# Delta-net projection by seven products: another order of the products, turned signs, and a bank of its own for two of them

## The chip, the cores and the metric

The kernel runs on one core of one Trainium2 chip. The number that counts is the device time of one execution in microseconds. A core has TensorE (matrix products, weight loads beside them), VectorE, ScalarE and GpSimd, and in the profile they are called PE (PEld for the weight loads), DVE, ACT and POOL. Products land in eight PSUM banks of 128 partitions and 512 fp32 numbers, called B[0] to B[7]; all else lies in SBUF. The engines wait for one another by counting semaphores.

## The reference

The kernel computes two blocks of a first model (a gated delta-net mixer and a retention mixer, each with a convolved feed-forward part) and a third block of another kind. The change touches only the delta-net mixer, and there the input projection of each of eight heads:

```python
def gated_deltanet(h, w_in, conv_w, a_log, dt_bias, norm_w, w_out):
    proj = h @ w_in                                  # h: 512 tokens x 1024
    qkv, z, a, bt = jnp.split(proj, ...)
    qkv = jax.nn.silu(causal_dwconv(qkv, conv_w))
    q, k, v = jnp.split(qkv, [H * dk, 2 * H * dk], axis=-1)
    ...                                              # decays, q and k normalised
    sol = lax.linalg.triangular_solve(kk + eye, rhs, lower=True, unit_diagonal=True)
    ...                                              # chunks of 64: state, output o
    o = o * lax.rsqrt(jnp.mean(o * o, ...) + 1e-6) * norm_w * jax.nn.silu(z)
    return o.reshape(b_, s, H * dv) @ w_out
```

All of it is fp32.

## The kernel before, in words

**The projection of a head.** A head needs four blocks of 128 output columns (q, k, v, z) of 1024 inputs for 512 tokens. They are made two at a time: pair (h, 0) is q and k, pair (h, 1) is z and v. A pair is a 2x2 product of blocks: weights A11, A12 (first block, lower and upper 512 inputs) and A21, A22 (second block), against the tokens' halves. Instead of eight block products it makes seven, M1 to M7, in Winograd's form. Each is four matmuls (128 inputs each) of 256 tokens. What the form needs beside them:

- sums of the weights, S1 to S4, which GpSimd makes in place in the ring of weight slots (`pool_gdn`; lines 2213, 2220, 2223 and 2225 are S3, S2, S1 and S4, 128x512 each);
- sums of the inputs, T1 to T4 (`gdn_T[0..3]`), made once by VectorE at the start (lines 1953 to 1964);
- copies of M1 and M7 out of their banks by ScalarE (`keep_m1` line 1694, `keep_m7` line 1701) and of the finished quarter C11 (`keep_c11`, line 1708), since M2 and M4 are added on top of M1 and M7 in the bank;
- the sums of the results by VectorE (`dve_pair`): t (line 1919), U2 (1926), c21 (1932), c22 (1937), c12 (1944).

**The order.** `GDN_ORDER` gives the order of the seven products; with four matmuls each a pair has steps 0 to 27 and a head 0 to 55. `pe_steps` issues a range of them and, at the first step of a product, the waits. The steps are not issued in one piece. They fill TensorE's gaps while it works on an earlier head, by hand-written positions:

- In the opening (`pe_gdn`, lines 1477 to 1542) pair (0,0) and (0,1) run among small products that make the gates, the first key sum (line 1510), the key products `kk` (1516), the transpose (1523), `qk` (1531) and `ktok` (1541). Steps 0 to 13 of pair (1,0) stand there too, the last two right in front of the head loop.
- In the head loop, each head h inverts its triangular matrix in six levels. A level is LD (line 1605), Tm on VectorE (2075), TE (line 1617), the inverse's update and transpose on VectorE (2091, 2093). Seven steps of head h+1 stand in each level, from step 14 on, split as `fill` says. So pair (h+1, 0) ends in level 2 and pair (h+1, 1) runs through levels 3 to 6.
- Then comes the state's recurrence over four pieces (lines 1653 to 1670: kv, wS, o) with the steps 0 to 13 of head h+2 between, as `ahead` says. VectorE makes vn (line 2170) and S (2184) for it, and between them it does convolution taps (1906), the next head's L (2016) and first D (2028, 2032).

The four columns of an adaLN product (`pe_ada`, line 256) stand in level 1 of every head but the first, in bank 7. ScalarE and VectorE have their orders written out as well (`act_gdn`, `dve_gdn`). GpSimd per head: S3 of the pairs (h+1,1) and (h+2,0), the other three of (h+1,1), one product on XT (line 2249), two decays, the other three of (h+2,0), and the query's product (2243). In the opening it waits, ahead of the sums of (1,0), for the first inverse of head 0 (VectorE, line 2041):

```python
            third(1, 0)
            decay(0)
            pool.wait_ge(dve_done, at("dve", "gdn", "inv", 0, 0))
            others(1, 0)
            query(0)
```

## Time and profile before

| what | us |
|---|---|
| device time, median of 3 runs | 2595.95 (2595.76 to 2597.06) |
| span of the profiled execution | 2595.1 |
| TensorE busy | 2532.1 (98%) |
| VectorE busy | 1643.4 (63%) |
| ScalarE busy | 719.3 (28%) |
| GpSimd busy | 252.9 (10%) |
| first and last start of a product of the pairs (line 1467) | 43.7 and 399.4 |
| one head of the loop (TensorE's line 1647, 164.70 to 211.85) | 47.15 |

The profiled execution is one execution; the page gives its span, which is 0.85 us under the median. The change touches the stage from some 40 to 402 us. A row of a timeline is a group of like instructions one after another: its start, the time from start to end, the engine and line of the kernel, what it writes and reads, and in brackets the time that the engine stood idle before it and what ended this.
### The profile page before, as it was taken

How to read it: one execution, taken by the hardware profiler on the slowest of the kernel's cores; microseconds unless marked ns; L12 is line 12 of the kernel's file. 1: busy time of each engine (PE TensorE's matmuls, PEld its weight loads, DVE VectorE, ACT ScalarE, POOL GpSimd, SP SyncE). 2: the span in 40 equal slices, each digit the busy share in tenths (PEclk: the TensorE clock that was granted, in tenths of full speed). 3: DMA queues.
4: the chain of work that ended last, by engine and by line, in shares of the span. 5: the costliest groups of instructions: out<-in, count | busy, mean ns of one | idle time of the engine just before them, and what ended most of it. 6: DMA issues, size and time to landing. Idle time of an engine off the chain costs nothing.

```text
span 2595.1 us, 32921 instructions
## 1 busy us (share of the span) xinstructions
PE 2532.1 (98%) x13038; PEld 1999.9 (77%) x13038; DVE 1643.4 (63%) x2905; ACT 719.3 (28%) x1381; POOL 252.9 (10%) x186
## 2 busy tenths in 40 slices
PE   6999999999999999999999999999999999999999
PEld 3777775688888888888888888886445568888888
DVE  2787875687776365455648777745375486666652
ACT  3555553321110122211203111004253375222200
POOL 1434331100000030000001000001121000000000
PEclk9999999999999999999999999999999999999999
DMA  8222311243433321122023453331021310212121
GB/s 350 109 79 74 131 74 72 91 185 146 188 142 144 120 77 70 69 83 84 33 97 130 163 195 148 137 122 69 33 83 65 130 66 33 93 70 98 67 90 55
DMA packets 26377, 276.81 MB, mean 107 GB/s; under 512 B 3689, under 2 KB 4585, under 8 KB 9201
## 3 DMA queue, kind: packets, MB, share of 16 engines
q1 hardware_dynamic: 23040, 268.92, 27.1%
q10 hardware_dynamic: 3184, 5.78, 0.7%
q8 instruction: 105, 1.72, 0.3%
q14 instruction: 48, 0.39, 0.0%
HBM read 272.58 MB, written 2.11 MB: 106 GB/s over the span
## 4 chain that ended last, share of the span: by engine, by line
PE 87%; DVE 7%; ACT 3%; DMA 2%; issue 1%; POOL 0%; SPq 0%; ACTq 0%; DVEq 0%; POOLq 0%
PE bank L688 29%; PE bank L772 15%; PE bank L2583 11%; PE bank L1467 5%; PE bank L2996 5%; PE bank L2369 4%; PE bank L419 3%; DVE arena L1906 1%; PE bank L2674 1%; DMA arena<-w_ada 1%; PE bank L501 1%; PE bank L2989 1%; PE bank L1617 1%; PE bank L1605 1%; PE bank L3139 1%
## 5 line engine op out<-in xcount | busy, mean ns | idle before, releaser
L688 PE MATMUL bank<-HT,ring 128*128 128x256 f32 x1056 | 248.0, 380 | 2.0 <-ACT HT L1104 2.0
L688 PE MATMUL bank<-arena,ring 128*128 128x256 f32 x1056 | 249.5, 379 | 0.0
L688 PE MATMUL bank<-arena 128*128 128x256 f32 x1056 | 249.5, 379 | 0.0
L688 PEld LDWEIGHTS bank<-HT,ring 128*128 128x128 f32 x1056 | 199.3, 190 | 34.2 <-issue 5.2
L688 PEld LDWEIGHTS bank<-arena,ring 128*128 128x128 f32 x1056 | 200.6, 190 | 27.3
L688 PEld LDWEIGHTS bank<-arena 128*128 128x128 f32 x1056 | 200.6, 190 | 27.3
L772 PE MATMUL bank<-arena,ring 128*128 128x256 f32 x936 | 207.0, 379 | 1.4 <-ACT arena L845 1.4
L772 PEld LDWEIGHTS bank<-arena,ring 128*128 128x128 f32 x936 | 177.4, 190 | 27.1 <-ACT arena L845 2.6
L1328 ACT ACTIVATE arena<-bank,ffc 128x512 f32<-128x512 f32 x66 | 51.3, 777 | 487.3 <-DVE bank L1234 487.3
L1133 POOL TENSOR_SCALAR XT<-XT,comb_v 128x512 f32<-128x512 f32 x32 | 50.1, 1577 | 1049.3 <-ACT HT L1104 652.3
L2996 PE MATMUL bank<-HT,ring 128*128 128x512 f32 x320 | 146.5, 598 | 0.5 <-ACT HT L1145 0.5
L1467 PE MATMUL bank<-arena,ring 128*128 128x256 f32 x512 | 133.2, 391 | 2.3 <-DVE arena L1964 0.8
L688 PE MATMUL bank<-HT,arena 128*128 128x256 f32 x528 | 125.5, 381 | 2.5 <-DVE arena L1289 2.4
L772 PE MATMUL bank<-arena 128*128 128x256 f32 x528 | 116.4, 379 | 0.0
L688 PEld LDWEIGHTS bank<-HT,arena 128*128 128x128 f32 x528 | 99.6, 190 | 18.7 <-DVE arena L1289 5.5
L2583 PE MATMUL bank<-arena,ring 128*128 128x256 f32 x512 | 112.7, 379 | 0.3 <-DVE arena L2789 0.3
L772 PEld LDWEIGHTS bank<-arena 128*128 128x128 f32 x528 | 100.3, 190 | 13.6
L2583 PEld LDWEIGHTS bank<-arena,ring 128*128 128x128 f32 x512 | 97.1, 190 | 15.3 <-issue 1.4
L394 DVE SCALAR_TENSOR_TENSOR arena<-ring,evec,arena 128x512 f32<-128x512 f32 x140 | 105.3, 752 | 2.9
L1467 PEld LDWEIGHTS bank<-arena,ring 128*128 128x128 f32 x512 | 90.3, 190 | 17.0 <-DVE arena L1964 1.2
L2996 PEld LDWEIGHTS bank<-HT,ring 128*128 128x128 f32 x320 | 57.2, 190 | 58.9 <-issue 56.8
L1244 DVE SCALAR_TENSOR_TENSOR arena<-bank,ffc,arena 128x511 f32<-128x511 f32 (+1 forms) x132 | 98.5, 746 | 3.5 <-ACT arena L1328 1.1
(509 smaller groups left out, 4403.5 us busy)
## 6 DMA issues: line engine op xcount, KB each, us to landing
ring<-w_ada SPq DMA_DIRECT2D x33, 2048.0 KB, 7.5
ring<-w_up SPq DMA_DIRECT2D x33, 2048.0 KB, 7.4
ring<-w_down SPq DMA_DIRECT2D x24, 1408.0 KB, 6.0
ring<-w_gdn SPq DMA_DIRECT2D x7, 2048.0 KB, 8.9
ring<-w_ret_qk SPq DMA_DIRECT2D x4, 2048.0 KB, 8.2
ring<-w_ret_v SPq DMA_DIRECT2D x4, 2048.0 KB, 8.2
ring<-w_ret_g SPq DMA_DIRECT2D x4, 2048.0 KB, 8.3
ring<-w_ret_out SPq DMA_DIRECT2D x4, 2048.0 KB, 8.3
```

The source lines that it names most:

```text
L394: ins = nc.vector.scalar_tensor_tensor(out=acc, in0=w[:, :, k, :], scalar=evec[:, e, k:k + 1], in1=acc, op0=ALU.mult, op1=ALU.add)
L419: ins = nc.tensor.matmul(B[bank][:, :], out_weights(pe, tag, n, k), src(k), start=(first and k == k0), stop=(last and k == k1 - 1))
L501: last = nc.tensor.matmul(bank[:, cols], out_weights(pe, tag, n, k), HT[:, k, cols], start=(k == 4), stop=(k == KC - 1))
L688: last = nc.tensor.matmul(out_, w[:, k, :], x[:, k, :], start=(first and k == 0), stop=(k == 3), skip_group_check=not first)
L772: last = nc.tensor.matmul(out_, w[:, k, :], x(k), start=(first and k == 0), stop=(k == KH2 - 1), skip_group_check=not first)
L1133: nc.gpsimd.tensor_scalar(XT[:, n, :], XT[:, n, :], comb_v[:, 2, n:n + 1], comb_v[:, 3, n:n + 1], ALU.mult, ALU.add)\
L1244: last = nc.vector.scalar_tensor_tensor(out=out_[:, m:], in0=src[:, 0:T - m], scalar=ffc[:, i, j, half, 2 - m:3 - m], in1=out_[:, m:], op0 ...
L1328: nc.scalar.activation(ffn_y[:, j % 2, :], up_bank(j)[:, :], ACT.Identity, scale=ffc[:, i, j, 0, 2:3], bias=ffc[:, i, j, 0, 3:4])\
L1467: last = nc.tensor.matmul(out_, w[:, k, :], x[:, k, :], start=(first and k == 0), stop=(k == 3), skip_group_check=not first)
L2369: last = nc.tensor.matmul(out_, w[:, k, :], x[:, k, :], start=(first and fresh and k == 0), stop=(k == 7), skip_group_check=not (first and ...
L2583: last = nc.tensor.matmul(out_, left, right, start=flag, stop=(k == 3), skip_group_check=not (first and fresh))
L2996: last = nc.tensor.matmul(bank[:, :], w[:, u, k, :], HT[:, k, :], start=(k == 0), stop=(k == KC - 1))
```

## The change

The seven products come in the order M1, M5, M2, M7, M6, M4, M3 (before: M1, M7, M2, M4, M5, M6, M3). Signs are turned: the weight sums and T1 to T4 are other sums and differences than before, and t, U2 and c12 subtract where they added, so that the four quarters come out the same. GpSimd now makes S1 first (A21 + A22, `lower_row`), which needs only the loaded weights, then S2 = A11 + S1 behind M1, S3 = S2 - A22 behind M5, and S4 behind M2. S2 lies where A11 was, and S1 and then S3 where A21 was.

M5 and M3 go to the upper half of bank 7 (`gdn_C`), where they were in the pair's own bank; M6 takes their old place. `pe_ada`, which also uses bank 7, moves from level 1 to level 3 (for all heads but the first and last) with a wait for the c12 of the next head. ScalarE's copies of M7 move back behind the later M7: behind `tokens` and behind the square of the key. In the opening `keep_c11(0)` goes ahead of `keep_m7(0, 0)`; `keep_m7(0, 1)` and GpSimd's list of calls stay where they were written.

```diff
         GDN_UNITS = ((0, 1), (3, 2))
-        GDN_ORDER = ("M1", "M7", "M2", "M4", "M5", "M6", "M3")
+        GDN_ORDER = ("M1", "M5", "M2", "M7", "M6", "M4", "M3")
+        gdn_C = B[7][:, TH:T]
...
                 Bg, Bx = B[p], B[1 - p]
+
+                def summed(which):
+
+                    pe.wait_ge(pool_done, at("pool", "gdn", which, h, p))
+
                 if name == "M1":
                     out_, w, x, first = Bg[:, 0:TH], A11, HT[:, 0:4, 0:TH], True
                     if k == 0:
@@ -1429,40 +1435,42 @@
                             slot_of(pe, ("gdn", h))
                         if h or p:
                             pe.wait_ge(dve_done, at("dve", "gdn", "c21", *pair_before(h, p)))
+                elif name == "M5":
+                    out_, w, x, first = gdn_C, A21, gdn_T[0], True
+                    if k == 0:
+                        if h or p:
+                            pe.wait_ge(dve_done, at("dve", "gdn", "c12", *pair_before(h, p)))
+                        else:
+                            pe.wait_ge(dve_done, at("dve", "gdn", "T1"))
+                        summed("S1")
+                elif name == "M2":
+                    out_, w, x, first = Bg[:, 0:TH], A12, HT[:, 4:8, 0:TH], False
+                    if k == 0:
+                        pe.wait_ge(act_done, at("act", "gdn", "m1", h, p))
                 elif name == "M7":
                     out_, w, x, first = Bx[:, 0:TH], A21, gdn_T[2], True
                     if k == 0:
                         if h == 0:
                             pe.wait_ge(dve_done, at("dve", "gdn", "T3"))
-                        if p:
-                            pe.wait_ge(dve_done, at("dve", "gdn", "c12", h, 0))
-                        elif h:
+                        if h and p == 0:
                             pe.wait_ge(act_done, at("act", "gdn", "z", h - 1))
-                        pe.wait_ge(pool_done, at("pool", "gdn", "S3", h, p))
-                elif name == "M2":
-                    out_, w, x, first = Bg[:, 0:TH], A12, HT[:, 4:8, 0:TH], False
+                        summed("S3")
+                elif name == "M6":
+                    out_, w, x, first = Bg[:, TH:T], A11, gdn_T[1], True
                     if k == 0:
-                        pe.wait_ge(act_done, at("act", "gdn", "m1", h, p))
+                        if h == 0:
+                            pe.wait_ge(dve_done, at("dve", "gdn", "T4"))
+                        if p == 0:
+                            pe.wait_ge(act_done, at("act", "gdn", "c11", h))
+                        summed("S2")
                 elif name == "M4":
                     out_, w, x, first = Bx[:, 0:TH], A22, gdn_T[3], False
                     if k == 0:
-                        if h == 0:
-                            pe.wait_ge(dve_done, at("dve", "gdn", "T4"))
                         pe.wait_ge(act_done, at("act", "gdn", "m7", h, p))
-                elif name == "M5":
-                    out_, w, x, first = Bg[:, TH:T], A11, gdn_T[0], True
+                else:
+                    out_, w, x, first = gdn_C, A12, HT[:, 4:8, TH:T], False
                     if k == 0:
-                        pe.wait_ge(pool_done, at("pool", "gdn", "S1", h, p))
-                        if p == 0:
-                            pe.wait_ge(act_done, at("act", "gdn", "c11", h))
-                elif name == "M6":
-                    out_, w, x, first = Bx[:, TH:T], A21, gdn_T[1], True
-                    if k == 0:
-                        pe.wait_ge(pool_done, at("pool", "gdn", "S2", h, p))
-                else:
-                    out_, w, x, first = Bg[:, TH:T], A12, HT[:, 4:8, TH:T], False
-                    if k == 0:
-                        pe.wait_ge(pool_done, at("pool", "gdn", "S4", h, p))
+                        summed("S4")
                         pe.wait_ge(dve_done, at("dve", "gdn", "t", h, p))
                 last = nc.tensor.matmul(out_, w[:, k, :], x[:, k, :], start=(first and k == 0), stop=(k == 3), skip_group_check=not first)
...
                     fill(l, 0, 1)
+                    if l == 3 and h and more:
+                        pe.wait_ge(dve_done, at("dve", "gdn", "c12", h + 1, 0))
+                        pe_ada(pe, 0, 3 + h)
                     pe.wait_ge(dve_done, at("dve", "gdn", "Tm", h, l))
                     pe.wait_ge(dve_done, at("dve", "gdn", "inv", h, l - 1))
                     for i in range(NT):
@@ -1632,7 +1643,6 @@
                     if l == 5 and more:
                         key_sum(h + 1)
                     if l == 1 and h and more:
-                        pe_ada(pe, 0, 3 + h)
                         osum(h - 1)
...
             nc.scalar.activation(S2[0:GH, :], B[3][0:GH, :], ACT.Relu, bias=gvec[0:GH, 2:3]).then_inc(act_done, AC.tick())
+            keep_c11(0)
             keep_m7(0, 0)
             act_root_tables()
             act.wait_ge(act_done, AC.n)
-            keep_c11(0)
...
             tap(0, 2)
-            keep_m7(1, 0)
             keep_c11(1)
             lower(0)
             for h in range(GH):
                 more = h + 1 < GH
                 tokens(h)
+                if more:
+                    keep_m7(h + 1, 0)
                 if h:
                     oroot(h - 1)
...
-                    keep_m7(h + 1, 1)
                     raw(h + 1)
                     silu(h + 1, 1)
                     square(h + 1, 1)
+                    keep_m7(h + 1, 1)
...
                         keep_m1(h + 2, 0)
-                        keep_m7(h + 2, 0)
                         keep_c11(h + 2)
...
-                nc.vector.tensor_tensor(gdn_t, Bg[:, TH:T], gdn_m7, ALU.add).then_inc(dve_done, DV.tick("gdn", "t", h, p))
+                nc.vector.tensor_tensor(gdn_t, gdn_m7, gdn_C, ALU.subtract).then_inc(dve_done, DV.tick("gdn", "t", h, p))
...
-                nc.vector.tensor_tensor(gdn_U2, Bx[:, TH:T], gdn_m1, ALU.add).then_inc(dve_done, DV.tick("gdn", "U2", h, p))
+                nc.vector.tensor_tensor(gdn_U2, Bg[:, TH:T], gdn_m1, ALU.subtract).then_inc(dve_done, DV.tick("gdn", "U2", h, p))
...
-                nc.vector.tensor_tensor(dst, Bg[:, TH:T], gdn_U2, ALU.add).then_inc(dve_done, DV.tick("gdn", "c12", h, p))
+                nc.vector.tensor_tensor(dst, gdn_C, gdn_U2, ALU.subtract).then_inc(dve_done, DV.tick("gdn", "c12", h, p))
...
-            nc.vector.tensor_tensor(gdn_T[2], HR[:, 4:8, :], HR[:, 0:4, :], ALU.subtract).then_inc(dve_done, DV.tick("gdn", "T3"))
-            nc.vector.tensor_tensor(gdn_T[0], HR[:, 0:4, :], HL[:, 0:4, :], ALU.subtract).then_inc(dve_done, DV.tick())
+            nc.vector.tensor_tensor(gdn_T[0], HL[:, 0:4, :], HR[:, 0:4, :], ALU.subtract).then_inc(dve_done, DV.tick("gdn", "T1"))
+            nc.vector.tensor_tensor(gdn_T[2], HR[:, 0:4, :], HR[:, 4:8, :], ALU.subtract).then_inc(dve_done, DV.tick("gdn", "T3"))
...
-            nc.vector.tensor_tensor(gdn_T[1], HR[:, 4:8, :], gdn_T[0], ALU.subtract).then_inc(dve_done, DV.tick())
+            nc.vector.tensor_tensor(gdn_T[1], HR[:, 4:8, :], gdn_T[0], ALU.add).then_inc(dve_done, DV.tick())
...
-            def third(h, p):
+            def lower_row(h, p):
 
                 A11, A12, A21, A22 = gdn_quarters(h, p)
                 if h == 0:
@@ -2210,19 +2220,19 @@
                 if h or p:
                     n = load_at[("gdn", h)]
                     pool.wait_ge(ring_full[n % SLOTS], landed(n))
-                nc.gpsimd.tensor_tensor(A21, A11, A21, ALU.subtract).then_inc(pool_done, PO.tick("gdn", "S3", h, p))
+                nc.gpsimd.tensor_tensor(A21, A21, A22, ALU.add).then_inc(pool_done, PO.tick("gdn", "S1", h, p))
 
             def others(h, p):
 
                 A11, A12, A21, A22 = gdn_quarters(h, p)
-                pool.wait_ge(pe_done, at("pe", "gdn", "M7", h, p))
-                pool.wait_ge(pool_done, at("pool", "gdn", "S3", h, p))
-                nc.gpsimd.tensor_tensor(A21, A22, A21, ALU.subtract).then_inc(pool_done, PO.tick("gdn", "S2", h, p))
+                pool.wait_ge(pool_done, at("pool", "gdn", "S1", h, p))
+                pool.wait_ge(pe_done, at("pe", "gdn", "M1", h, p))
+                nc.gpsimd.tensor_tensor(A11, A11, A21, ALU.add).then_inc(pool_done, PO.tick("gdn", "S2", h, p))
                 pool.wait_ge(pool_done, at("pool", "gdn", "S2", h, p))
-                pool.wait_ge(pe_done, at("pe", "gdn", "M1", h, p))
-                nc.gpsimd.tensor_tensor(A11, A11, A21, ALU.add).then_inc(pool_done, PO.tick("gdn", "S1", h, p))
+                pool.wait_ge(pe_done, at("pe", "gdn", "M5", h, p))
+                nc.gpsimd.tensor_tensor(A21, A11, A22, ALU.subtract).then_inc(pool_done, PO.tick("gdn", "S3", h, p))
                 pool.wait_ge(pe_done, at("pe", "gdn", "M2", h, p))
-                nc.gpsimd.tensor_tensor(A12, A12, A21, ALU.subtract).then_inc(pool_done, PO.tick("gdn", "S4", h, p))
+                nc.gpsimd.tensor_tensor(A12, A12, A11, ALU.add).then_inc(pool_done, PO.tick("gdn", "S4", h, p))
...
-            third(0, 0)
+            lower_row(0, 0)
             others(0, 0)
-            third(0, 1)
+            lower_row(0, 1)
             others(0, 1)
-            third(1, 0)
+            lower_row(1, 0)
             decay(0)
             pool.wait_ge(dve_done, at("dve", "gdn", "inv", 0, 0))
             others(1, 0)
             query(0)
             for h in range(GH - 1):
-                third(h + 1, 1)
+                lower_row(h + 1, 1)
                 if h + 2 < GH:
-                    third(h + 2, 0)
+                    lower_row(h + 2, 0)
                 others(h + 1, 1)
```

The places at which it shows on the engines are these. First TensorE right in front of the head loop, in the opening: the last transposes of `ktok`, two steps of pair (1,0), and LD of level 1 of head 0. Before:

```order
L1541 MATMUL bank<-ident,arena 128x128 x3
L1467 MATMUL bank<-arena,ring 128x256 [waits act_done]
L1467 MATMUL bank<-arena,ring 128x256
L1605 MATMUL bank<-arena 64x64 [waits act_done,dve_done]
L1605 MATMUL bank<-arena 64x64 x7
```

Now (1541 is line 1549 there, 1467 is 1475, 1605 is 1613):

```order
L1549 MATMUL bank<-ident,arena 128x128 x3
L1475 MATMUL bank<-arena,ring 128x256 [waits pool_done,act_done]
L1475 MATMUL bank<-arena,ring 128x256
L1613 MATMUL bank<-arena 64x64 [waits act_done,dve_done]
L1613 MATMUL bank<-arena 64x64 x7
```

The two products ahead of LD are steps 12 and 13: M4 before, M7 now, with a wait for GpSimd that was not there.

Second, TensorE in a head, from level 1 to TE of level 3. Before:

```order
L1467 MATMUL bank<-arena,ring 128x256 x4
L256 MATMUL bank<-ones,arena 128x1 x4
L1559 MATMUL bank<-arena,ones 128x512
L1605 MATMUL bank<-arena 64x64 x8
L1467 MATMUL bank<-arena,ring 128x256 x3
L1617 MATMUL bank<-arena 64x64 x8
L1467 MATMUL bank<-HT,ring 128x256 x4
L1605 MATMUL bank<-arena 64x64 x8
L1552 MATMUL bank<-ident,arena 128x128 x4
L1467 MATMUL bank<-HT,ring 128x256 x3
L1617 MATMUL bank<-arena 64x64 x8
```

Now:

```order
L1475 MATMUL bank<-arena,ring 128x256 x4
L1567 MATMUL bank<-arena,ones 128x512
L1613 MATMUL bank<-arena 64x64 x8
L1475 MATMUL bank<-arena,ring 128x256 x3
L1628 MATMUL bank<-arena 64x64 x8
L1475 MATMUL bank<-HT,ring 128x256 x4
L1613 MATMUL bank<-arena 64x64 x8
L1560 MATMUL bank<-ident,arena 128x128 x4
L1475 MATMUL bank<-HT,ring 128x256 x3
L256 MATMUL bank<-ones,arena 128x1 x4
L1628 MATMUL bank<-arena 64x64 x8
```

The four small products of line 256 have moved two levels on, to just ahead of TE (1617, now 1628).

Third, GpSimd in the opening, from the first sum of pair (1,0). Before:

```order
L2213 TENSOR_TENSOR ring<-ring 128x512 [waits ring_full1]
L2231 TENSOR_TENSOR arena<-arena,causal 128x512 [waits act_done,masks_in]
L2234 TENSOR_TENSOR arena<-arena,causal 128x512 [waits act_done]
L2220 TENSOR_TENSOR ring<-ring 128x512 [waits pool_done,pe_done,dve_done]
L2223 TENSOR_TENSOR ring<-ring 128x512 [waits pe_done,pool_done]
L2225 TENSOR_TENSOR ring<-ring 128x512 [waits pe_done]
```

Now:

```order
L2223 TENSOR_TENSOR ring<-ring 128x512 [waits ring_full1]
L2241 TENSOR_TENSOR arena<-arena,causal 128x512 [waits act_done,masks_in]
L2244 TENSOR_TENSOR arena<-arena,causal 128x512 [waits act_done]
L2230 TENSOR_TENSOR ring<-ring 128x512 [waits pe_done,pool_done,dve_done]
L2233 TENSOR_TENSOR ring<-ring 128x512 [waits pe_done,pool_done]
L2235 TENSOR_TENSOR ring<-ring 128x512 [waits pe_done]
```

The rows stand in the same places, but they are other sums: before S3, (decays), S2, S1, S4; now S1, (decays), S2, S3, S4.

## Rows read from the trace of the kernel before

**Rows 1.** the page, part 1: busy us of each engine (share of the span)

```profile
PE 2532.1 (98%) x13038; PEld 1999.9 (77%) x13038; DVE 1643.4 (63%) x2905; ACT 719.3 (28%) x1381; POOL 252.9 (10%) x186
```

**Rows 2.** waits of TensorE, 38 to 412 us: us in total, times, longest

```profile
PE bank L1617 <- DVE arena L2075: 7.7, 7, 1.1
PE bank L1660 <- DVE arena L2184: 5.4, 7, 0.9
```

**Rows 3.** timeline of TensorE, opening: start, us, what, [idle before <-releaser]

```profile
60.05 1.97 PE L1467 MATMUL bank<-arena,ring 128*128 128x256 f32 x8 [0.59 <-DVE arena L1944]
...
78.08 1.16 PE L1516 MATMUL bank<-arena 128*128 128x128 f32 x8 [1.10 <-DVE arena L2004]
...
84.40 1.03 PE L1467 MATMUL bank<-arena,ring 128*128 128x256 f32 x4
...
88.26 2.43 PE L1467 MATMUL bank<-arena,ring 128*128 128x256 f32 x10 [0.54 <-POOL ring L2223]
```

**Rows 4.** timeline of ScalarE, opening

```profile
63.12 1.28 ACT L1778 ACT_TABLE_LOAD   x1
...
67.06 0.63 ACT L1790 ACTIVATE arena<-arena 128x512 f32<-128x512 f32 x1
69.06 0.60 ACT L1757 ACTIVATE arena<-bank 128x512 f32<-128x512 f32 x1 [1.37 <-PE bank L1503]
...
76.49 0.63 ACT L1800 ACTIVATE arena<-arena 128x512 f32<-128x512 f32 x1
```

**Rows 5.** timeline of VectorE, opening

```profile
77.15 0.88 DVE L2004 TENSOR_TENSOR arena<-arena 128x512 f32<-128x512 f32 x1 [1.42 <-ACT arena L1800]
...
80.58 0.87 DVE L2028 TENSOR_TENSOR arena<-arena,maskL 64x256 f32<-64x256 f32 x2
```

**Rows 6.** timeline of GpSimd, opening

```profile
85.59 1.28 POOL L2220 TENSOR_TENSOR ring<-ring 128x512 f32<-128x512 f32 x1 [8.11 <-DVE arena L2041]
86.94 1.26 POOL L2223 TENSOR_TENSOR ring<-ring 128x512 f32<-128x512 f32 x1
```

**Rows 7.** timeline of TensorE, one head

```profile
167.79 1.03 PE L1467 MATMUL bank<-HT,ring 128*128 128x256 f32 x4
...
175.00 0.49 PE L1660 MATMUL bank<-arena 128*128 128x128 f32 x2 [0.86 <-DVE arena L2184]
...
202.49 0.68 PE L1617 MATMUL bank<-arena 64*64 64x64 f32 x16 [1.11 <-DVE arena L2075]
```

**Rows 8.** timeline of VectorE, one head

```profile
168.94 0.75 DVE L1906 SCALAR_TENSOR_TENSOR arena<-sel,gconv,arena 128x511 f32<-128x511 f32 x1 [0.55 <-ACT arena L1717]
169.60 0.28 DVE L2170 TENSOR_TENSOR arena<-arena,bank 128x128 f32<-128x128 f32 x1
...
171.98 2.58 DVE L2028 TENSOR_TENSOR arena<-arena,maskL 64x256 f32<-64x256 f32 x2
...
199.33 2.77 DVE L1906 SCALAR_TENSOR_TENSOR arena<-arena,gconv 128x511 f32<-128x511 f32 x2
```

**Rows 9.** timeline of GpSimd, one head

```profile
171.60 1.27 POOL L2220 TENSOR_TENSOR ring<-ring 128x512 f32<-128x512 f32 x1 [6.28 <-PE bank L1467]
...
198.81 1.72 POOL L2225 TENSOR_TENSOR ring<-ring 128x512 f32<-128x512 f32 x1
```

**Rows 10.** stretches: busy us of each engine, granted clock, DMA

```profile
403.34:406.75 3.41, 1.42 (x9) 1.07 (x9) 2.87 (x8) 1.40 (x3) 0.00 (x0) 1.00 1.00 428
406.75:413.58 6.83, 6.81 (x19) 4.70 (x20) 4.13 (x13) 0.60 (x1) 0.00 (x0) 0.50 0.65 278
...
2096.34:2099.75 3.41, 3.41 (x25) 2.72 (x26) 3.31 (x14) 2.82 (x10) 0.00 (x0) 0.50 0.70 298
```

**Rows 11.** timeline of VectorE, c12 in level 3 of one head

```profile
191.45 0.42 DVE L1944 TENSOR_TENSOR arena<-bank,HT 128x256 f32<-128x256 f32 x1
```

**Rows 12.** timelines of GpSimd and VectorE, two that start together

```profile
67.56 1.28 POOL L2213 TENSOR_TENSOR ring<-ring 128x512 f32<-128x512 f32 x1
...
67.58 1.29 DVE L1992 TENSOR_SCALAR arena<-arena 128x32 f32<-128x32 f32 x1
```

## The prediction

> **What bounds the kernel.** First the busy line of the page [rows 1]: TensorE works 2532.1 of 2595.1 us, so a change is worth what it does to the 63 us in which TensorE does nothing. Then its waits in the delta-net stage, 38 to 412 us [rows 2]: seven of up to 1.1 us for line 2075 (the mask product of a level), seven of up to 0.9 us for line 2184 (the state), and single ones. Last the timelines of each engine, in the opening (46 to 92 us) and in one head that stands for six (164 to 212 us). The opening is bound by waits in both directions. In a head TensorE stands still twice: before line 1660 at 175.00 (0.86 us) and before line 1617 at 202.49 (1.11 us) [rows 7]. In both VectorE is late, and it is late because GpSimd's weight sums hold it up (steps 6 and 7). A head takes 47.15 us, about 2 of them in these waits.
>
> The counts of instructions are the same on every engine: 56 steps of four products a head, four sums a pair, the same copies. So all that can change is what waits for what. Steps of a pair are counted 0 to 27 here.
>
> **1. The copy m7 in the opening: +2.2 us.** ScalarE copies M7 of pair (0,1) in front of a table load, the key's silu and its square. M7 was the second product, and the table load behind its copy ran at 63.12 [rows 4]. Now M7 is the fourth: M5 takes the place at 60.05 [rows 3], then the eight small steps (62 to 64.3), M2, and M7 ends near 68.2 (60.05, plus 0.2 for a later softplus, plus 1.8 M5, 2.4 small steps, 1.8 M2, 1.9 M7). From there: copy 0.4, table load 1.28, silu and square 0.63 each, about 3.0 us, so line 1757 starts at 71.2 and not 69.06 [rows 4]. From line 1757 on ScalarE has no gap up to the end of line 1800 at 77.12, and line 2004 (0.88 us) and TensorE's line 1516 at 78.08 hang on it [rows 3, 5]. TensorE waited 1.1 us there already [rows 3], so nothing covers the delay: 1516 starts at about 80.25. The wait of 0.59 us ahead of it, at 60.05 [rows 3], loses or gains nothing in the end, since TensorE waits at 1516 in any case.
>
> **2. M7 of pair (1,0) behind two GpSimd sums: +3.9, and -0.5 back.** Ahead of the head loop TensorE takes steps 12 and 13 of pair (1,0). They were M4, which needs no sum, and ran at 84.40. Now they are M7, which waits for S3. GpSimd makes S2 and S3 only after its wait for the first inverse of head 0 (line 2041, the releaser in the row): before, line 2220 started at 85.59 and 2223 ended at 88.20 [rows 6]. All of this stands 2.2 later by step 1: sums from 87.8 to 90.4, while TensorE arrives at 86.6. It waits 3.9 us, and everything queued behind M7 on TensorE, the levels of head 0 from line 1605 (85.36) on, waits with it. Step 16 used to wait 0.54 us for line 2223 at 88.26 [rows 3]; that sum is then long made: -0.5. Together with step 1: +5.6.
>
> **3. Clock: +1.1 (0 to 3.4).** Such gaps cost more than themselves. From 403.34 to 406.75 TensorE was busy 1.42 of 3.41 us at a granted clock of 1.00 (2.4 GHz), and the next 6.83 us stood at 0.50 (1.2 GHz) at full work[rows 10]. In the new opening it does nothing from 77.2 to 80.25 and from 86.6 to 90.5, more than in the first of these rows. A fall of 3.4 us, as at 2096 [rows 10], partly inside the wait itself, halves the clock over about 2.2 us of work: 1.1 lost. The lower end is no fall, the upper one 6.8 us at half clock, 3.4 lost.
>
> **4. The fall at 406.75: -1.7 (0 to -3.4).** It cost 6.83/2 = 3.4 us. The same gaps come later by some 5 us against whatever sets the moment of a fall. The other fall in the rows, at 2096, lasted 3.4 us [rows 10]; that is the nearest row, so I take half.
>
> **5. Ada's four matmuls: 0 (-0.1 to +0.3).** Line 256 (0.8 us, 183.05) goes from level 1 to level 3, ahead of the line 1617 that stood at 192.03. Everything from 183.05 to there starts 0.8 earlier, then it is paid. The added wait is for c12 of the next head. VectorE's queue ahead of it also moves up: U2 no longer waits for M6, c12 (191.45 to 191.87 [rows 11]) ends near 191.06, and TensorE comes for it at 191.2. If c12 came late, the levels behind it would pay, hence the upper end.
>
> **6. The wait at line 1660: 0 (-5.2 to +1).** It comes from line 2028 (twice, 2.58 us at 171.98), which has two arena inputs; with GpSimd idle the same two took 0.87 us [rows 8, 5]. GpSimd's three sums followed one another there from 171.60 on, to 175.7 [rows 9], since S2 waited for M7. Now S2 waits only for M1, whose last product starts at 167.79 and ends at 168.82: S2 starts at 168.90. VectorE's line 1906 started at 168.94 [rows 8], and it also reads two SBUF tensors. Who is first? GpSimd by 0.04 us. In the one row pair with so small a lead GpSimd started at 67.56 and VectorE at 67.58, and VectorE took 1.29 us and ended after GpSimd [rows 12]. So 1906 ends at about 170.7 and not 169.69, line 2170 (169.60) comes 1.0 later, and TensorE, which came for it at 169.97, waits 1.0 us. Behind that the sums leave line 2028 alone (S3 at 172.6 to 173.9 stops it once, S4 starts at 175.2), line 2184 is ready at 174.9, and TensorE is at 1660 at 175.0 as before. The wait has moved by 5 us, its size has not. The lower end is all six of 0.86.
>
> The Trainium skill, SBUF — State Buffer, section "Who interferes with whom", says that a VectorE instruction with two SBUF inputs and a GpSimd instruction that reads SBUF exclude each other for a whole instruction, and that the order of issue decides who is blocked. By that rule this term is 0; were the port only shared, the sum would be 5.2 lower. The rows agree with exclusion: line 2028 took three times as long under the sums, and line 1992 ended 0.04 us behind the sum that had started 0.03 ahead of it.
>
> **7. The wait at line 1617: -1.4 (-7.7 to +1).** VectorE does line 1906 three times ahead of it, and two of them, in 2.77 us from 199.33, are stopped by S4 (198.81) [rows 8, 9] and the XT product behind it. Now S2 starts at 193.4 and not 195.96, S3 at 196.0, S4 at 198.5. They stop the first tap at 193.6 and line 394 at 196.3, where VectorE had 1.2 us of waits to lose, so line 2091 comes only 0.2 late (197.6). Its tap of 198.44 is just ahead of S4, which then runs to 200.3, and the last two taps end near 201.9: 0.2 earlier. Seven heads by 0.2 is 1.4. If S4 is first, it is 0.
>
> **Sum.** The profiled execution spans 2595.1; the median of the runs is 2595.95, 0.85 more, and I add to the median: +2.2 +3.9 -0.5 +1.1 -1.7 +0 +0 -1.4 = +3.6, so 2599.5 us. 0.2% of this kernel is 5.2 us, about what its measurement can tell from no change.
>
> **Rivals.**
> Slower: the clock decides. After two gaps within 13 us at the opening it falls twice or for 6.8 us (3.4 lost, not 1.1), and the fall at 407 stays whole (0, not -1.7). +5.6 +3.4 -1.4 = +7.6, 2603.5. For it: the 6.83 us row, and that 3.9 us of nothing is longer than any gap before that fall. Against: at 2096 it was 3.4. It decides from the second 3.4 us on at half clock. Even one of the two parts makes 2601 or more. Chance 0.34.
> VectorE wins the race at 168.94: line 1906 ends on time, S2 ends at 170.8, the second tap and line 2184 come 0.3 late, and the wait at 175.00 is gone: six times 0.54. +3.6 -3.2 = 2596.3. For it: 0.04 us is little. Chance 0.13.
> Faster: the earlier sums free VectorE at both places. Six times 0.86 and seven times 1.1 are -12.9; with +5.6 +1.1 = -6.2, 2589.8. Against: GpSimd's work is as long as before and VectorE has two-input work at nearly all times. Chance 0.04.
> The opening is paid only in part (another path of ScalarE, or a sum earlier than I read it): 2596 to 2598. Chance 0.05, within my range.
>
> **Numbers.** My forecast has 0.44, its own range is 2597 to 2601; with the others, 2596 to 2604. Faster by over 0.2% 0.04; slower by over 0.2% 0.36 (the clock rival and a bit of the forecast's upper end); within 0.2% 0.60.
>
> **What would show it.** Step 1: TensorE's first product of khat (line 1516 before) at about 80.3, with a gap of 3 us ahead. Step 2: a gap near 3.9 us before a product of the pair's helper at 90 to 91, released by GpSimd, and the first LD of a level (line 1605 before) at 91 to 92. Step 3: rows at 0.50 near 90. Step 4: the row after 403 to 412. Step 6: a wait of 1.0 us at line 1668's successor, released by 2170's, and none at 1660's. Step 7: waits of 0.9 and not 1.1 at 1617's. A head of 46.9 to 47.2 us; one of 45.2 would prove the third rival. I am wrong if no gap stands before M7 of pair (1,0), or if the heads change by over 0.5 us each.

## The result, and the profile after

The changed kernel takes 2604.97 us (median of 7 runs, 2603.34 to 2605.46), the kernel before 2597.06 in the same comparison (7 runs, 2595.76 to 2599.81). The ratio is 1.003, 95% interval 1.0019 to 1.0041: slower by 0.3%, and 1 us outside the range of the prediction. The prediction started from a median of 2595.95, 1.1 us under the one that the kernel before has here. A second comparison of the same two kernels gave 1.0032 (1.002 to 1.0045). The profiled execution takes 2603.81 us with a span of 2602.0, which is 6.9 more than before.

The busy line first. TensorE works 2533.5 us and not 2532.1 [rows 1], so of the 6.9 us only 1.4 are work that runs longer, and 5.5 are new idle time.

```profile
PE 2533.5 (97%) x13038; PEld 2000.3 (77%) x13038; DVE 1646.6 (63%) x2905; ACT 718.7 (28%) x1381; POOL 247.4 (10%) x186
```

The waits of TensorE from 38 to 420 us name the new idle time (line, releaser: us in total, times, longest). Beside [rows 2]: the wait for the mask product still comes seven times, six times with 1.1 us and once, in head 0, with 0.6 (lines 1628 and 2085 are 1617 and 2075 of before), the one for the state (line 2184 then, 2194 now) has nearly gone, one of the same size stands before line 1678 (1668 then) for vn (2180, then 2170), and two long single ones are new.

```profile
PE bank L1628 <- DVE arena L2085: 7.3, 7, 1.1
PE bank L1678 <- DVE arena L2180: 6.4, 8, 0.9
PE bank L1475 <- POOL ring L2233: 3.8, 1, 3.8
PE bank L1524 <- DVE arena L2014: 2.9, 1, 2.9
PE bank L1670 <- DVE arena L2194: 0.7, 2, 0.4
```

TensorE's timeline in the opening, which answers to [rows 3], shows the two single waits:

```profile
79.86 1.16 PE L1524 MATMUL bank<-arena 128*128 128x128 f32 x8 [2.92 <-DVE arena L2014]
90.01 2.05 PE L1475 MATMUL bank<-arena,ring 128*128 128x256 f32 x4 [3.77 <-POOL ring L2233]
91.99 1.12 PE L1613 MATMUL bank<-arena 64*64 64x64 f32 x16
98.02 0.68 PE L1613 MATMUL bank<-arena 64*64 64x64 f32 x16
```

The row at 90.01 is M7 of pair (1,0); two fp32 matmuls took 2.05 us there, and the like of them took 1.10 in other runs below. The reason stands in the stretches (us, busy time of each engine with its count, granted clock, DMA), which answer to [rows 10]:

```profile
84.86:88.28 3.42, 1.39 (x13) 1.15 (x11) 1.54 (x4) 2.87 (x10) 1.01 (x1) 1.00 0.00 0
88.28:95.11 6.83, 5.10 (x26) 3.35 (x28) 1.88 (x3) 0.17 (x1) 6.40 (x6) 0.50 0.01 2
1904.17:1907.59 3.42, 3.42 (x7) 1.60 (x6) 2.12 (x5) 2.10 (x3) 1.11 (x1) 0.50 0.35 149
```

The clock falls in the gap before M7 and stays at 1.2 GHz for 6.83 us, in which TensorE works for 5.10. The fall at 406.75 of before is not there, and one of 3.4 us at 1904 is new.

To see where the 6.9 us arise, I subtracted the start of each TensorE instruction before from the start of the same one after (both have 13038 of them). The difference is a running account ("LD" is the first product of a level of the inverse; the second LD is that of level 2 of head 0):

| TensorE instruction (start before) | after minus before, us |
|---|---|
| first of khat (78.08) | +1.8 |
| M7 of (1,0), now in M4's place (84.40) | +5.6 |
| first LD of a level (85.36) | +6.6 |
| second LD (90.61) | +7.4 |
| head 1 (164.70) | +7.1 |
| head 6 (400.55) | +8.1 |
| 452.7, behind the fall of before | +5.9 |
| 1890 | +5.3 |
| 1910 | +6.9 |
| last | +6.9 |

### The profile page after: what moved, and what is told of

It is laid out like the page before. It is cut to its first block, busy times and chain, and to the rows that moved or that the text cites. A ratio compares the mean times of both kernels' runs of the same rounds, so it can differ in the third digit from the quotient of the medians.

```text
span 2602.0 us, 32934 instructions
## 1 busy us (share of the span) xinstructions
PE 2533.5 (97%) x13038; PEld 2000.3 (77%) x13038; DVE 1646.6 (63%) x2905; ACT 718.7 (28%) x1381; POOL 247.4 (10%) x186
## 4 chain that ended last, share of the span: by engine, by line
PE 87%; DVE 7%; ACT 3%; SPq 1%; issue 1%; DMA 1%; POOL 0%; ACTq 0%; DVEq 0%; POOLq 0%
PE bank L688 30%; PE bank L772 15%; PE bank L2593 11%; PE bank L1475 5%; PE bank L3006 5%; PE bank L2379 4%; PE bank L419 3%; DVE arena L1916 2%; PE bank L2684 1%; PE bank L501 1%; PE bank L2999 1%; PE bank L1628 1%; PE bank L3149 1%; PE bank L2675 1%; PE bank L1613 1%
```

## The experiments

Each is an edit of the changed kernel unless it says otherwise. Where only one time was taken, the profile is what is read; the kernel before ran beside each: its median was 2595.66 us (13 runs) beside experiments 1, 2, 5 and the first of 3, 2596.53 (3) beside 6 to 9, and 2596.45 (27) beside 4, 10 and the second of 3.

**1. GpSimd's sums of (1,0) without the wait for the first inverse.**

```diff
-            pool.wait_ge(dve_done, at("dve", "gdn", "inv", 0, 0))
             others(1, 0)
```

> GpSimd's wait for the first inverse of head 0, ahead of the sums of pair (1,0), is removed. Theory A (the 3.77 us in front of M7 of pair (1,0) are GpSimd's order of work, and the long gap brings the clock down for the 6.83 us from 88.28): M7 no longer waits, LD of head 0 starts 3.8 to 4 us earlier than in the changed kernel, no row at 0.50 stands near 90, and with the 1 us of work that this saves at half clock the offset against before at that LD is 1.0 to 2.0 and not 7.4. End: 5.0 to 5.6 us under the changed kernel if the fall near 406 stays away, about 2.5 to 3.4 less of a gain if it comes back at some later place. Theory B (the wait is only in the way: M7 would wait for something else, such as M5 of its own pair or VectorE): the gap moves by under 1 us and the time stays within 1 us of the changed kernel.

Measured: 2600.45 us (10 runs, 2600.05 to 2603.89), ratio 1.0019 (1.0009 to 1.0028). In TensorE's timeline M7 of (1,0) is at 88.58 with no wait, and the second LD is 5.1 us behind the kernel before and not 7.4:

```profile
88.58 1.03 PE L1475 MATMUL bank<-arena,ring 128*128 128x256 f32 x4
```

The wait was GpSimd's order of work, as theory A says. But a part of it comes back: the sums now stand beside VectorE's first masks, and TensorE waits 1.48 us for line 2085 (the second row is VectorE's, two mask products that take 0.87 us in the changed kernel at 85.86):

```profile
92.77 0.68 PE L1628 MATMUL bank<-arena 64*64 64x64 f32 x16 [1.48 <-DVE arena L2085]
88.36 2.11 DVE L2048 TENSOR_TENSOR arena<-arena,maskL 64x256 f32<-64x256 f32 x2 [4.16 <-ACT arena L1822]
```

The clock fell all the same, ten us earlier, in and behind the gap of 2.92 us that the first product of khat still has:

```profile
78.62:85.45 6.83, 5.99 (x20) 5.16 (x21) 3.18 (x8) 2.65 (x4) 2.27 (x3) 0.50 0.38 163
```

So the offset of 1.0 to 2.0 that I had expected was not reached: there was no row at 0.50 near 90, but the time at half clock had only moved. This profiled execution is the slowest of the ten, and its span (2602.1) is that of the changed kernel. The ratios (1.0019 against 1.003) put the edit's gain at 0.11% of the kernel, some 3 us and not the 5.0 to 5.6 expected; their intervals overlap (1.0009 to 1.0028 and 1.0019 to 1.0041).

**2. The copy of M7 of pair (0,1) later.**

```diff
-            keep_m7(0, 1)
             silu(0, 1)
             square(0, 1)
+            keep_m7(0, 1)
```

> ScalarE's copy of M7 of pair (0,1) goes behind the key's silu and square. Theory A (the copy delays them): the first product of khat starts at 78.1 to 78.4 and not 79.86, its wait is 1.1 and not 2.9 us, and all behind it is 1.5 to 1.8 us earlier; the gap before M7 of pair (1,0) stays near 3.8 since GpSimd and TensorE both come earlier. Theory B (the key chain is late for another reason, VectorE's taps or sums of the pair being later because M7 is later): 1516's successor stays within 0.3 us of 79.86, since VectorE's sum of the pair then waits for the later copy.

Measured: one time, 2599.88 us. The first product of khat is back at the place of before, with the wait of before, and the 3.77 us ahead of M7 stand unchanged, so step 1 of the prediction is this copy and nothing else:

```profile
77.71 1.16 PE L1524 MATMUL bank<-arena 128*128 128x128 f32 x8 [1.10 <-DVE arena L2014]
87.86 1.10 PE L1475 MATMUL bank<-arena,ring 128*128 128x256 f32 x4 [3.77 <-POOL ring L2233]
```

**3. The waits filled with work.**

```diff
+            for _ in range(14):
+                nc.tensor.matmul(B[5][:, 0:P], ident[:, :], ident[:, :], start=True, stop=True)
             pe_steps(pe, 1, 12, GDN_AHEAD[-1])
```

> 14 extra products of 128 columns (their result is read by nothing) stand in front of M7 of pair (1,0), so that TensorE works through the wait of 3.77 us. What is computed stays. Theory A (the gap brings the clock down, and the fall costs 2 to 2.4 us there): no row at 0.50 in 84 to 96, M7 starts at 90.0 as before, and the second LD (98.02 in the changed kernel) comes 1.6 to 2.4 us earlier; the gain is kept to the end or given back by a fall at another place. Theory B (the fall has nothing to do with the gap, it comes by time or from the opening before 80): the row at 0.50 stays near 88, and the time stays within 0.5 us.

Measured: one time, 2603.02 us. The 14 products take 3.29 us, M7 waits 0.66 more and starts at 89.64 (90.01 in the changed kernel, whose first product of khat is also 0.4 us later), now at full clock (1.10 us and not 2.05):

```profile
85.69 3.29 PE L1581 MATMUL bank<-ident 128*128 128x128 f32 x28
89.64 1.10 PE L1475 MATMUL bank<-arena,ring 128*128 128x256 f32 x4 [0.66 <-POOL ring L2235]
87.83:94.66 6.83, 6.17 (x59) 4.93 (x58) 3.22 (x6) 0.63 (x2) 6.68 (x6) 1.00 0.00 0
412.10:418.93 6.83, 6.76 (x19) 4.73 (x20) 4.20 (x13) 0.60 (x1) 0.00 (x0) 0.50 0.66 281
```

The fall near 88 is gone. Measured from the first product of khat on, the second LD comes 3.3 us later than before and not 5.6: the fall cost 2.3 us. The last row is the other half of the answer: a fall of 6.83 us stands at 412 again, as in the kernel before, and the single time is only 2 us under the changed kernel's.

The same with both waits filled (11 more products ahead of khat), timed in three rounds:

> The changed kernel with 11 more products (their result is read by nothing) in the wait of 2.9 us ahead of the first product of khat, and 14 in the wait of 3.77 us ahead of M7 of pair (1,0): TensorE works through both waits, which keep their length. Theory A (the falls between 78 and 95 come from these waits and cost 2.3 to 3.9 us): no row at 0.50 between 44 and 400, the second LD 4.5 to 4.9 us behind the kernel before, and a median 2.3 to 3.9 us under that of the changed kernel in the same call, unless the fall near 412 comes in more of its runs. Theory B (the clock falls at times of its own): a row at 0.50 stands between 75 and 100 all the same, and the medians agree within 0.7 us.

Measured: 2602.57 us (10 runs), ratio 1.0023 (1.0014 to 1.0032), beside 2604.66 of the changed kernel taken with it. No row at 0.50 between 33 and 411, and again one near 412:

```profile
76.79:94.66 17.87, 16.73 (x137) 14.87 (x136) 7.75 (x18) 8.17 (x19) 9.78 (x8) 1.00 0.25 104
411.31:418.14 6.83, 6.61 (x22) 5.21 (x23) 4.28 (x14) 0.60 (x1) 0.00 (x0) 0.50 0.82 350
```

The difference of the medians is 2.1 us, just under the 2.3 to 3.9 expected. The intervals of the two ratios overlap, though the slowest of these ten times (2603.20) is under the fastest of the five (2603.29). Since the falls behind the opening differ too, the size of this one is read from the profiles: here too the second LD is 3.3 us later than before, counted from the first product of khat (5.0 in all, where 4.5 to 4.9 was expected). The median is still 0.23% over the kernel before, so the waits themselves, 1.8 and 3.8 us, cost more than the clock.

The fourteen profiles together bear out that gaps bring the fall. All six with the unfilled gap of 3.77 us have a fall between 78 and 97 us. Of the three in which a gap of 2.9 us ahead of khat is the longest (experiments 1, 7 and the first of this one), two have one. The five with no such gap (the kernel before, experiments 9 and 10 and the second of this one) have none.

**4. The changed kernel once more.**

> The changed kernel once more, as it is. Theory A (the work is the same from run to run, the falls of the clock are not): every wait of over 1 us stands as in the first profile within 0.1 us, but the rows at 0.50 are others (one or two between 78 and 96, with or without one near 412); the median is 7 to 9 us over the kernel before. Theory B (the falls belong to fixed places of the program): the rows at 0.50 are the same as in the first profile: 6.83 us from 88.3, none near 412, 3.4 us near 1904.

Measured: 2604.66 us (5 runs, 2603.29 to 2606.37), ratio 1.0032 (1.002 to 1.0045). Theory A is wrong and theory B holds: the falls are those of the first profile, 6.83 us from 87.83, none near 412, 3.4 us at 1903.7.

```profile
87.83:94.66 6.83, 5.10 (x26) 3.35 (x28) 1.89 (x3) 0.17 (x1) 6.39 (x6) 0.50 0.01 2
```

Yet three other kernels whose opening is this one's to the instruction (experiments 5, 6 and 8) fell differently in it: 3.4 us at 80.96 and 3.4 at 91.20; 3.4 at 79.18 and 6.83 at 89.42; 6.83 at 88.67. Their second LD, counted again from the first product of khat, comes 6.4, 7.2 and 6.0 us later than before. Against the 3.3 without a fall that is a price of 2.3 to 3.9 us for the opening's falls over four kernels. Experiment 2, with the same gap and a single fall of 3.4 us (at 88.89), has 4.8: a price of 1.5.

**5. VectorE's tap ahead of the sum.** ScalarE makes the tap's product before the next head's gate:

```diff
-                    gate(h + 1)
                     tap(h + 1, 2)
+                    gate(h + 1)
```

> ScalarE makes the product for the convolution tap ahead of the gate of the next head, so VectorE's tap of line 1916 can start ahead of GpSimd's S2. Theory A (the wait for vn at line 1678, 0.9 us in six heads, is VectorE blocked for one whole instruction by an S2 that starts just before it): with the tap first, the wait at 1678 falls to under 0.3 us, S2 starts up to 0.9 us later, and a head takes 46.5 to 46.9 us and not 47.37. Theory B (the wait is the sum of work on VectorE and only its place depends on who is first): the wait comes back at line 1670 or at 1628 with 0.5 to 0.9 us, and a head stays within 0.2 us of 47.37.

Measured: one time, 2597.56 us; a head takes 46.20 us, below the 46.5 to 46.9 expected. First VectorE and GpSimd of the changed kernel, then of this one:

```profile
176.08 1.85 DVE L1916 SCALAR_TENSOR_TENSOR arena<-sel,gconv,arena 128x511 f32<-128x511 f32 x1 [0.55 <-ACT arena L1727]
177.85 0.28 DVE L2180 TENSOR_TENSOR arena<-arena,bank 128x128 f32<-128x128 f32 x1
176.12 1.27 POOL L2230 TENSOR_TENSOR ring<-ring 128x512 f32<-128x512 f32 x1 [3.64 <-PE bank L1475]
178.18 0.49 PE L1678 MATMUL bank<-arena 128*128 128x128 f32 x2 [0.91 <-DVE arena L2180]
```

```profile
174.85 0.74 DVE L1916 SCALAR_TENSOR_TENSOR arena<-sel,gconv,arena 128x511 f32<-128x511 f32 x1
175.62 0.29 DVE L2180 TENSOR_TENSOR arena<-arena,bank 128x128 f32<-128x128 f32 x1
175.51 1.27 POOL L2230 TENSOR_TENSOR ring<-ring 128x512 f32<-128x512 f32 x1 [3.64 <-PE bank L1475]
176.51 0.38 PE L1678 MATMUL bank<-arena 128*128 128x128 f32 x2
```

The tap took 1.85 us beside the sum of line 2230 and 0.74 ahead of it, and TensorE's 0.91 us are gone. In the changed kernel the records start the tap 0.04 us ahead of the sum (0.03 to 0.04 in all six heads), and the tap is still the one that waits, ending behind it.

**6. The sum behind the tap.** From the third head on, S2 of pair (h,0) waits longer:

```diff
-                pool.wait_ge(pe_done, at("pe", "gdn", "M1", h, p))
+                pool.wait_ge(pe_done, at("pe", "gdn", "M5" if h > 1 and p == 0 else "M1", h, p))
```

> GpSimd's S2 of the pairs (h,0) from the third head on waits for M5 of its pair and not for M1, so it starts some 1.1 us later than in the changed kernel. Theory A (VectorE is blocked for a whole instruction by a sum that starts just ahead of it, and the place of TensorE's wait follows that race): VectorE's tap of line 1916 is first, the wait for vn at line 1678 (0.91 us) falls under 0.2, and the sums run into the two products of line 2038 instead, so 0.3 to 0.9 us come back at line 1670; a head of 46.4 to 47.4 us. Theory B (the wait at line 1678 comes from the new order of TensorE's products, not from GpSimd): it stays at 0.9.

Measured: one time, 2603.86 us, a head of 47.23. The tap takes 0.75 us, the wait at 1678 is gone and the same size stands at 1670, where the kernel before had it, behind two mask products of 2.65 us together:

```profile
177.07 0.75 DVE L1916 SCALAR_TENSOR_TENSOR arena<-sel,gconv,arena 128x511 f32<-128x511 f32 x1 [0.55 <-ACT arena L1727]
180.12 2.65 DVE L2038 TENSOR_TENSOR arena<-arena,maskL 64x256 f32<-64x256 f32 x2
183.19 0.49 PE L1670 MATMUL bank<-arena 128*128 128x128 f32 x2 [0.92 <-DVE arena L2194]
179.80 1.27 POOL L2230 TENSOR_TENSOR ring<-ring 128x512 f32<-128x512 f32 x1 [6.33 <-PE bank L1475]
```

**7. The sums made thin.** Each of the four weight sums adds one column of 128 (the output is then not the reference's); waits and order stay:

```diff
-                nc.gpsimd.tensor_tensor(A11, A11, A21, ALU.add)
+                nc.gpsimd.tensor_tensor(A11[:, :, 0:1], A11[:, :, 0:1], A21[:, :, 0:1], ALU.add)
```

> The four weight sums are cut to one column of 128, so that GpSimd hardly works in them while every wait and their order stay (the output is then not the reference's: only one column of each summed weight block is summed). Theory A (both waits of a head, 0.91 at line 1678 and 1.11 at line 1628, are VectorE held up by the sums): both fall under 0.4, a head takes 45.2 to 45.7 us and not 47.37; the wait of 3.77 us in the opening falls by some 2.5 us, since two sums of 1.27 us lie in it. Theory B (VectorE's own queue is too long): a head stays over 46.8.

Measured: one time, 2584.97 us. A head takes 44.85 us, 2.5 less than in the changed kernel and less than the 45.2 to 45.7 expected; the waits before lines 1628 and, but for the last head, 1678 have left the list of waits, and the opening's wait for GpSimd falls to 1.7 us. The two products of line 2038, 2.65 us above, take 0.86:

```profile
172.05 0.86 DVE L2038 TENSOR_TENSOR arena<-arena,maskL 64x256 f32<-64x256 f32 x2
171.73 0.21 POOL L2233 TENSOR_TENSOR ring<-ring 128x4 f32<-128x4 f32 x1 [2.51 <-PE bank L1475]
```

Both waits of a head are thus VectorE held up by GpSimd's sums, and 2.5 us is what the sums cost a head.

**8. One tap from level 4 to level 5.**

```diff
-                            dve_taps(dve, h + 1, 0, 1, 3)
+                            dve_taps(dve, h + 1, 0, 1, 2)
...
-                            dve_taps(dve, h + 1, 0, 3, 4)
+                            dve_taps(dve, h + 1, 0, 2, 4)
```

> One of VectorE's three taps ahead of the mask product of level 5 goes behind the inverse of level 5 (all else as in the changed kernel). Theory A (the 1.11 us at line 1628 are VectorE's queue, lengthened by S4 and the XT product): line 2085 of level 5 comes 0.75 us or more earlier, the wait at 1628 falls to 0.1 to 0.4, the tap finds room in VectorE's idle time of 1.8 us in level 5, and a head takes 46.4 to 46.7 us. Theory B (the tap delays the copy of the last transpose or the silu of the next head, so the time is paid again at line 1615 or 1518): a head stays over 47.0.

Measured: one time, 2600.57 us; the wait at 1628 falls to 0.3 as expected, and a head takes 46.6. But line 1670 has a wait for the state's first copy in six heads. Waits of TensorE:

```profile
PE bank L1670 <- DVE arena L2191: 4.7, 6, 2.2
PE bank L1628 <- DVE arena L2085: 2.0, 6, 0.3
```

**9. The kernel before with experiment 5's edit.**

> The kernel before with ScalarE's product for the tap ahead of the gate, as in the run on the changed kernel that took 0.97 us out of every head. In the kernel before VectorE was late at line 1660 and not at 1668, and GpSimd's S2 came long behind the tap. Theory A (the tap's start gains only where a sum can block it): the wait at 1660 stays at 0.6 to 0.9 us and a head within 0.3 us of 47.15. Theory B (the earlier tap alone is the gain, in any order of products): the wait at 1660 falls under 0.3 and a head takes 46.5 or less; then the changed order of products has no part in the gain.

Measured: one time, 2594.92 us, a head of 47.06. TensorE's wait at line 1660 is still 0.86 and line 2028 still 2.58 [rows 7, 8]. The tap was never blocked there, so its earlier start is worth 0.08 us a head. The 1.17 that the same edit takes out of a head in experiment 5 (47.37 to 46.20, which is 0.94 under the kernel before) are to be had only with the changed order.

```profile
174.38 0.49 PE L1660 MATMUL bank<-arena 128*128 128x128 f32 x2 [0.86 <-DVE arena L2184]
171.36 2.58 DVE L2028 TENSOR_TENSOR arena<-arena,maskL 64x256 f32<-64x256 f32 x2
```

**10. A version faster than both.** Experiments 1, 2 and 5 in one kernel:

> The changed kernel with three edits together: no wait of GpSimd for the first inverse, the copy of M7 of pair (0,1) behind the key's square, ScalarE's product for the tap ahead of the gate. Theory A (the loss is the opening, the gain is only the six waits at 1678): the second LD of head 0 stands 1.2 to 2.2 us behind that of the kernel before, each of six heads gains 0.94, so 3.5 to 4.4 us ahead at 400 us, and the end 2 to 5 us under the kernel before by what the falls of the clock do (up to 3.4 us each way): ratio 0.998 to 0.9993. Theory B (the clock takes back what is gained in the delta-net stage): ratio 0.9995 to 1.001.

Measured: 2589.31 us (10 runs, 2588.02 to 2592.26), ratio 0.9974 (0.9965 to 0.9984). It is faster than the kernel before by 0.26%, more than the 0.07 to 0.2% that theory A gave. TensorE's list of waits has no row for GpSimd's sums of (1,0) and none for vn but two, 0.7 us together:

```profile
PE bank L1628 <- DVE arena L2085: 8.8, 8, 1.5
PE bank L1678 <- DVE arena L2180: 0.7, 2, 0.5
```

Its second LD stands 0.6 us behind the kernel before and not 1.2 to 2.2 (the clock does not fall in this opening), a head takes 46.2, and at 400 us it is 5.5 ahead. No fall stands near 406, which is 2.8 more; at 1900 some 1.6 of it goes back.

With experiment 8's edit too:

> The same three edits, and one of VectorE's taps moved from level 4 to level 5, which by itself took the wait at 1628 from 1.11 to 0.3 but brought 0.2 to 0.7 us at line 1670 in some heads. Theory A (the two edits work at two places and add up): a head takes 45.5 to 45.9 us, 8 to 10 us under the kernel before at 400 us, ratio 0.9965 to 0.998. Theory B (with both, VectorE's queue is late at line 1670 and keeps the head at 46.2): ratio like that of the three edits alone, within 0.0005.

Measured: 2590.63 us (11 runs), ratio 0.998 (0.9971 to 0.9989). That is 0.0006 above the three edits alone, just over the 0.0005 of theory B, and theory A is out: a head takes 46.58 us, 0.4 more than without the fourth edit. Its waits of TensorE again have line 1670 with 4.7 us. The chain of it, in VectorE's, GpSimd's and TensorE's timelines:

```profile
207.80 1.49 DVE L2014 TENSOR_TENSOR arena<-arena 128x512 f32<-128x512 f32 x1
213.40 1.68 DVE L1916 SCALAR_TENSOR_TENSOR arena<-sel,gconv,arena 128x511 f32<-128x511 f32 x1
207.46 1.28 POOL L2241 TENSOR_TENSOR arena<-arena,causal 128x512 f32<-128x512 f32 x1 [7.87 <-ACT arena L1777]
213.27 1.27 POOL L2230 TENSOR_TENSOR ring<-ring 128x512 f32<-128x512 f32 x1 [2.85 <-PE bank L1475]
213.63 0.46 PE L1670 MATMUL bank<-arena 128*128 128x128 f32 x2 [0.51 <-DVE arena L2191]
```

The khat product of line 2014 (0.69 us in the kernel of three edits) now meets GpSimd's decay product, ends 0.8 later, and at 213.40 the tap is behind the sum again. The 0.8 us that the moved tap freed at line 1628 are taken back, and more, behind these two new collisions.

## Why the prediction was wrong

The sum was +3.6, the profile says +6.9. Three steps failed: step 3 (the length of the clock's fall, 1.2 us short), step 6 (the balance of the heads, 1.2) and step 7 (what the earlier sums give back, 0.9); a term of 1.6 us is missing besides. By its steps:

- **Step 1** (+2.2): +1.85, from 60.05 to the first product of khat. Experiment 2 removes just that. Right, 0.35 too high.
- **Step 2** (+3.9 and -0.5): the wait is 3.77 (my own 86.6 and 90.4 make 3.8), and with the clock left whole (experiment 3) M7's place to the second LD gives the 0.5 back. Right; experiment 1 adds that the sums, put earlier, hold up VectorE for 1.5 us.
- **Step 3** (+1.1, 0 to 3.4): failed. I took a fall of 3.4 us from the row at 2096 against the one of 6.83 at 406.75, though the new gap was longer than anything ahead of either. It lasted 6.83 in two profiles and cost 2.3 us, and the falls of the three kernels with the same opening cost 2.6 to 3.9. The gap's length alone does not set that of the fall: behind the same 3.77 us it lasted 3.4 us in experiments 2 and 5. The rival "slower" had this half of it right, with 3.4 us for what cost 2.3, and the other half wrong: the fall at 407 did not stay.
- **Step 4** (-1.7): -2.2, the fall at 406 is not there (8.1 at 404, 5.9 at 453; two short waits for VectorE that it had covered come back). The size is near, and that is luck: I took half between a fall and none. The stretch ahead of the place is as empty as before, beside [rows 10], and the clock held:

```profile
411.45:414.86 3.41, 1.43 (x9) 1.08 (x9) 2.87 (x8) 1.40 (x3) 0.00 (x0) 1.00 1.02 437
414.86:421.69 6.83, 5.86 (x35) 4.50 (x36) 4.13 (x13) 1.79 (x4) 1.21 (x1) 1.00 0.64 276
```

  What decides it is not shown. That the new fall took its place is no rule: experiments 1, 2, 6 and 8 had both, experiments 9 and 10 neither.
- A term is missing: a fall of 3.4 us at 1904, +1.6. The stretch ahead of it, first of before and then of after, is equally empty, and in the kernel before the clock held behind it too:

```profile
1894.95:1898.37 3.42, 1.56 (x12) 0.41 (x10) 3.42 (x7) 0.63 (x1) 1.38 (x1) 1.00 1.05 450
1900.76:1904.17 3.41, 1.55 (x11) 0.46 (x10) 3.41 (x7) 0.78 (x2) 1.37 (x1) 1.00 0.97 418
```

The fall came in nine of the twelve later profiles, among them experiment 9, where the products have their old order. So the change does not need to be there for it, and with a single profile of before that lacks it the forecast had no such term. Why the clock fell in one kernel and held in the other stays open. Between 530 and 1890 the offset goes from 5.9 to 5.3, which I can't ascribe.
- **Step 5** (0): right. The offset changes by 0.03 over the four ada products and what they passed.
- **Step 6** (0): failed in its balance. The place and size of the wait are right, 0.91 for 1.0, with the sum as its cause (experiments 5 and 6). In part that is luck: I had the sum start 0.04 us ahead of the tap and took the outcome from one row pair [rows 12], whose VectorE instruction has a single input; the records have the tap 0.04 us ahead. But the balance is not 0. TensorE also comes to line 1670 0.13 us late at 182.35 (1.00 us behind the product ahead of it, where the other pieces have 0.87), and 0.91 + 0.13 less 0.86 is most of the 0.2 by which each of six heads grows (47.37 us, above the 46.9 to 47.2 that I had named): +1.2. I had written that TensorE is at this line "as before", and it was not.
- **Step 7** (-1.4): failed. It is -0.5, in head 0 alone, where the wait is 0.6 and not 1.1; in the others it stays 1.1. I gave the tap ahead of S4 the start and named the other case (0). The rows of VectorE and GpSimd show that other case:

```profile
205.94 1.73 DVE L1916 SCALAR_TENSOR_TENSOR arena<-wab,gconv,arena 128x509 f32<-128x509 f32 x1
205.86 1.26 POOL L2235 TENSOR_TENSOR ring<-ring 128x512 f32<-128x512 f32 x1 [1.20 <-PE bank L1475]
209.86 0.68 PE L1628 MATMUL bank<-arena 64*64 64x64 f32 x16 [1.11 <-DVE arena L2085]
```

Added up: 1.85 + 3.8 - 0.5 + 2.3 - 2.2 + 1.2 - 0.5 - 0.6 + 1.6 = 6.9. Of the 3.3 us by which I was off, the clock's falls (steps 3, 4 and the one at 1904) are 2.3, steps 6 and 7 are 2.1, and step 1 and the drift take 1.0 back. The medians differ by 7.9 and 8.2, a little more than the profiles. In every run with both numbers the device time is 1.8 us above the span of the same execution. So the profile of before (span 2595.1) is of an execution of some 2596.9 us, near the median of 2597.06, and the one of the changed kernel (2603.81) is 1.2 under its own. Of the 5.5 us between my 2599.5 and 2604.97, 3.3 are thus the steps, 1.1 the median of before, which was 2595.95 in the runs I started from, and 1.1 the place of the two profiles among their runs.

The rival "faster" priced both waits of a head at 2 us; experiment 7 shows 2.5 if the sums cost nothing. It was right that the waits are the sums', and wrong that their earlier place frees VectorE. The rival in which VectorE wins the race at the tap did not come, but experiment 5 makes it come: a head is then 0.94 us shorter than before, where I had 0.54.

The Trainium skill, SBUF — State Buffer, section "Who interferes with whom", speaks of exclusion by whole instructions. The rows agree: 1.85 us for a tap that takes 0.74, 2.65 for two products that take 0.86. As to who is blocked, the section has the order of issue decide. The record of the tap starts at 176.08, that of the sum at 176.12, and the tap is the one that lost; so the rule can't be checked where two starts are within 0.04 us. At 205.86 and 205.94 the first, GpSimd, did win. So did the first with the larger leads of VectorE's tap in experiment 5 (174.85 against 175.51) and of GpSimd's sum in experiment 6 (179.80 against 180.12).

## What to carry to other kernels

When an order is changed, look first at the helpers whose own order was written for the old one: here three edits (a copy moved, a wait of GpSimd taken out, a product of ScalarE moved) turned +0.3% into -0.26%. Where VectorE and GpSimd both read SBUF, busy times don't tell; list who starts first at each meeting, and look for an edit on a third engine that shifts one of the two, as one ScalarE product did for 1.2 us a head. A gap that a new order puts into TensorE's work is priced with its length and then the clock, by the longest fall in the trace and not the nearest one: behind the gap of 3.77 us it was the longest in four profiles of six.

## What the runs showed of the hardware

The falls of the clock were not the same where the instructions were. One opening had three patterns in four kernels that differ only behind it (6.83 us twice; 3.4 and 3.4; 3.4 and 6.83), while the same kernel profiled twice repeated its falls to within 0.5 us.

A long fall can be cheap. In experiments 5, 7 and the first of 10 one lasted 10.24 us near 2090, three times that of the kernel before [rows 10], and cost 0.7 to 0.8 us more. A wait for VectorE lies in it, which the slower work ahead of it filled: the rows are TensorE's product behind that wait, in the kernel before and in experiment 5.

```profile
2095.72 1.76 PE L3499 MATMUL bank<-ident,arena 128*128 128x128 f32 x8 [2.72 <-DVE arena L3703]
```

```profile
2095.57 1.97 PE L3509 MATMUL bank<-ident,arena 128*128 128x128 f32 x8 [1.52 <-DVE arena L3713]
```
